# Latent attention in another order: 512 latent columns token tile by token tile, rope keys under the norm, values behind the scores

## The chip, the cores and the metric

The kernel runs on one core of one Trainium2 chip. The metric is the device time of one execution in microseconds (us), lower is better. Three runs of the kernel before took 2278.98, 2285.95 and 2294.7 us, median 2285.95. All work is in fp32: a product with a weight is written as three matmuls on split operands, so that the weights need two passes of other engines before they can be used.

## The reference

Two stacks of transformer layers stand behind each other, over 256 tokens of width 1024. The change touches one mixer alone, the latent attention (MLA) in the third layer of the second stack, between one MLP and the next:

```python
H, dqk = MLA_HEADS, MLA_NOPE + MLA_ROPE            # 8 heads, 128 + 64
c_q, c_kv, k_pe = jnp.split(x @ w_in, [384, 384 + 256], axis=-1)
q = (rms_norm_2(c_q, q_norm_g) @ w_uq).reshape(B, S, H, dqk)
q = jnp.concatenate([q[..., :MLA_NOPE], rope(q[..., MLA_NOPE:], positions)], -1) * (dqk ** -0.5)
kv = (rms_norm_2(c_kv, kv_norm_g) @ w_ukv).reshape(B, S, H, MLA_NOPE + MLA_V)
k_nope, v = kv[..., :MLA_NOPE], kv[..., MLA_NOPE:]
k_pe = rope(k_pe[:, :, None, :], positions)
...
s = jnp.einsum('bqhd,bkhd->bhqk', qi, k)           # causal mask, softmax, then p @ v
return o.reshape(B, S, H * MLA_V) @ w_o            # 1024 x 1024
```

The result is added to ALPHA times the layer's input and goes through a layer norm, whose output the next MLP reads.

## The kernel before

Every engine has its own program, written out by hand; the order in it is the order of execution, and semaphores join the engines. 256 tokens are two token tiles of 128 (`tt`).

**Weights.** Five slots of 128 x 2048 fp32 go round as a ring. SyncE (SP) loads them in one queue, in the order of use, each as soon as PE has released the slot's user five places earlier (`slot_free`). ScalarE (ACT) writes a rounded copy `slot_hi` (L1242), VectorE (DVE) the remainder `slot_lo` (L1612), and only then may PE read it. Both engines do that in line with their other work, at calls of `weights.ahead(u)`: everything up to three slots past `u` is split there, and an engine that comes to it before the load has landed waits, with all that stands behind it.

**Banks.** PE writes into four PSUM banks, also a ring. The order of `bank(...)` calls in `plan()` says which product gets which bank; a bank can be opened only when its user four places earlier has been read out. Sums of down projections go into a separate accumulator `acc`.

**Products.** `product` (L676) is three matmuls: hi x hi, hi x lo, lo x hi. A matmul has 256 or 512 columns. `transposes` and the like (L674) are PE transposes against the identity. PE's `wait` and `in_sbuf` first let the array run empty if a slot is still to be released.

**The latent attention before.** The input projection's 640 latent columns and 64 rope columns come as three slots `mw`: number 2 (192 columns and the rope columns twice), then 0 and 1 (256 columns each). `head` does 2 and 0 token tile by token tile, because the layer norm ahead delivers them so; then PE makes the rope keys feature-major (`mk`), then number 1 (`token_major`). ACT copies all three banks, squares, and DVE scales 384 and 256 columns (L2222 to L2229) in one go. PE transposes five latent tiles (`mc`), DVE multiplies them by the gain into `mcg` (L2236), ACT rounds (L1570), DVE subtracts (L2242): `mcT`. Then four slots `muq` give queries (`mq` 0 to 3 plain, 4 and 5 rope), two slots `mukv` keys and values (`mkv`). DVE turns the rope parts in `exchanged` (L2073 to L2076) straight out of the bank, which holds that bank. Then 8 heads' scores (`ms`), mask and maximum on DVE (L1682 to L1688), exponentials on ACT (L1303), transposes of the probabilities (`mp`), probabilities x values (`my`), division on DVE (L2278), transposes `mt`, and the output projection `mwo` into `acc`. `project` does the first slot over both token tiles and the last three token tile by token tile, so that the next layer norm can start on tile 0; between them stand that norm's transposes (`ln_turned`).

In SP's queue the two tables of the next layer norm (L586) stand between `mw` and `muq`; they wait until the layer norm ahead is over.

## Time and profile before

| what | value |
|---|---|
| runs | 2278.98, 2285.95, 2294.7 us |
| profiled execution | 2281.16 us, of it span 2279.4 us |
| PE busy | 2163.3 us, 95% of the span |
| DVE, ACT, POOL busy | 1394.7, 1095.3, 140.3 us |
| mean granted TensorE clock | 0.984 |
| DMA | 378.10 MB, mean 166 GB/s |

The latent attention lies between about 1554 us and 1694 us of the span. To read it: look at a stretch's granted clock first (1.00 is 2.4 GHz, 0.50 is 1.2 GHz), then at how much of the stretch PE was busy, then at who ended PE's idle time. A share of busy time over the whole span says little here, since all but this stretch runs nearly without gaps.

### The profile page before, as it was taken

What the parts mean: (1) busy time and instruction counts of PE and PEld (TensorE: products, weight loads), DVE (VectorE), ACT (ScalarE), POOL (GpSimd) and SP (SyncE); (2) the same over time, 40 slices, a digit from 0 to 9 for tenths busy, and PEclk for the clock granted to TensorE, in tenths of its full rate; (3) what the DMA queues carried; (4) which work ended last, traced back from release to release, by engine and by line L of the source; (5) the groups of instructions that cost most, each with busy time, mean ns of one, the idle gap of its engine ahead of it and who ended that gap; (6) DMA issues with size and microseconds to landing.
All of it is one profiled execution on the core that took longest, in us unless ns stands there. A gap on an engine that the chain in (4) does not pass through costs nothing.

```text
span 2279.4 us, 33795 instructions
## 1 busy us (share of the span) xinstructions
PE 2163.3 (95%) x14753; PEld 1991.5 (87%) x14759; DVE 1394.7 (61%) x1477; ACT 1095.3 (48%) x1254; POOL 140.3 (6%) x82
## 2 busy tenths in 40 slices
PE   7998999999999999999999889997889999999998
PEld 6988899899889999988998879997679989988997
DVE  5856677675667666555655676555546557465654
ACT  4565555546545543444544654443335434354443
POOL 1000010020001003100000100000000003000000
PEclk9999999999999999999999999998899999999999
DMA  7423555563345555554555545563325565445553
GB/s 234 158 93 130 166 185 194 166 199 93 111 167 174 187 166 194 163 167 160 191 185 185 188 131 185 185 205 114 111 94 184 187 202 184 163 154 178 185 185 130
DMA packets 273292, 378.10 MB, mean 166 GB/s; under 512 B 13957, under 2 KB 236410, under 8 KB 273146
## 3 DMA queue, kind: packets, MB, share of 16 engines
q1 hardware_dynamic: 272236, 374.57, 50.3%
q8 instruction: 117, 1.92, 0.4%
q10 hardware_dynamic: 910, 1.38, 0.2%
q14 instruction: 29, 0.24, 0.0%
HBM read 374.87 MB, written 1.05 MB: 165 GB/s over the span
## 4 chain that ended last, share of the span: by engine, by line
PE 80%; DVE 7%; ACT 4%; DMA 3%; DVEq 2%; issue 1%; PEld 1%; SPq 1%; POOL 0%; ACTq 0%; PEldq 0%; POOLq 0%
PE bank L676 51%; PE acc L676 27%; DVE slot_lo L1612 3%; PE bank L674 2%; DVEq L1607 2%; ACT slot_hi L1242 1%; DMA slot<-in_w_in 1%; PEld bank L676 1%; DMA slot<-in_lru_w_in 1%; ACT arena L1237 1%; SPq L551 0%; DVE arena L2168 0%; DVE split L1645 0%; ACT split L1270 0%; DVE arena L1951 0%
## 5 line engine op out<-in xcount | busy, mean ns | idle before, releaser
L1612 DVE TENSOR_TENSOR slot_lo<-slot,slot_hi 128x2048 fp32r<-128x2048 f32 (+1 forms) x344 | 807.0, 2351 | 436.7 <-ACT slot_hi L1242 435.7
L676 PE MATMUL bank<-split,slot_hi 128*128 128x256 f32 x5496 | 1008.5, 286 | 15.3 <-ACT arena L1237 5.6
L676 PEld LDWEIGHTS bank<-split,slot_hi 128*128 128x128 f32 x5496 | 869.0, 193 | 29.5 <-issue 10.7
L1242 ACT ACTIVATE slot_hi<-slot 128x2048 fp32r<-128x2048 f32 (+1 forms) x344 | 653.0, 1902 | 303.4 <-DMA slot<-in_mlp_w 145.5
L676 PE MATMUL bank<-split,slot_lo 128*128 128x256 f32 x2748 | 781.1, 284 | 0.0
L676 PE MATMUL acc<-slot_hi,split 128*128 128x512 f32 x1904 | 610.4, 393 | 16.7 <-DVE split L2207 8.3
L676 PEld LDWEIGHTS bank<-split,slot_lo 128*128 128x128 f32 x2748 | 530.9, 193 | 0.0
L676 PEld LDWEIGHTS acc<-slot_hi,split 128*128 128x128 f32 x1904 | 359.8, 189 | 95.8 <-issue 8.5
L676 PE MATMUL acc<-slot_lo,split 128*128 128x512 f32 x952 | 373.1, 392 | 0.0
L676 PE MATMUL bank<-slot_hi,split 128*128 128x256 f32 (+1 forms) x1648 | 309.1, 287 | 20.6 <-DVE split L1645 11.7
L1237 ACT ACTIVATE arena<-bank 128x512 f32<-128x512 f32 (+1 forms) x194 | 108.8, 574 | 391.3 <-PE bank L676 359.8
L676 PEld LDWEIGHTS bank<-slot_hi,split 128*128 128x128 f32 x1648 | 262.5, 194 | 25.4 <-DVE split L1645 14.6
L676 PE MATMUL bank<-slot_lo,split 128*128 128x256 f32 (+1 forms) x824 | 236.0, 286 | 0.0
L676 PEld LDWEIGHTS acc<-slot_lo,split 128*128 128x128 f32 x952 | 180.0, 189 | 34.1
L676 PEld LDWEIGHTS bank<-slot_lo,split 128*128 128x128 f32 x824 | 159.9, 194 | 0.8
L676 PE MATMUL bank<-arena 128*128 128x64 f32 (+7 forms) x596 | 112.1, 353 | 18.1 <-ACT arena L1237 8.2
L676 PEld LDWEIGHTS bank<-arena 128*128 128x128 f32 (+2 forms) x596 | 80.3, 202 | 41.9 <-issue 30.6
L2005 DVE TENSOR_TENSOR arena<-arena 128x512 f32<-128x512 f32 x64 | 44.2, 691 | 112.3 <-ACT arena L1237 112.1
L1951 DVE SCALAR_TENSOR_TENSOR arena<-bank,par,arena 128x254 f32<-128x254 f32 (+1 forms) x176 | 76.7, 478 | 52.4 <-ACT arena L1407 49.1
L1407 ACT ACTIVATE arena<-bank,par 128x256 f32<-128x256 f32 x88 | 44.8, 560 | 97.5 <-PE bank L676 92.7
L1703 DVE TENSOR_TENSOR split<-arena,split 128x512 fp32r<-128x512 f32 x86 | 59.0, 686 | 26.7 <-ACT split L1417 20.4
L674 PE MATMUL bank<-con,arena 128*128 128x128 f32 x302 | 46.3, 301 | 21.7 <-DVE arena L1799 8.7
(194 smaller groups left out, 1038.5 us busy)
## 6 DMA issues: line engine op xcount, KB each, us to landing
slot<-in_mlp_w SPq DMA_DIRECT2D x128, 1024.0 KB, 5.4
slot<-in_ret_w_in SPq DMA_DIRECT2D x48, 1024.0 KB, 5.2
slot<-in_w_up SPq DMA_DIRECT2D x44, 1024.0 KB, 5.1
slot<-in_w_in SPq DMA_DIRECT2D x42, 1024.0 KB, 5.3
slot<-in_w_down SPq DMA_DIRECT2D x22, 1024.0 KB, 5.0
slot<-in_ret_w_o SPq DMA_DIRECT2D x16, 1024.0 KB, 5.1
slot<-in_lru_w_in SPq DMA_DIRECT2D x10, 1024.0 KB, 8.1
slot<-in_w_out SPq DMA_DIRECT2D x8, 1024.0 KB, 6.1
```

The lines of the kernel that those rows point to most:

```text
L674: i = nc.tensor.transpose(o, w, ident)
L676: i = nc.tensor.matmul(o, w, m, start=start, stop=stop)
L1237: return A(o, i, func, **kw).then_inc(bank_read[u.r], 1)
L1242: A(whi[u.r][:, 0:u.cols], raw[u.r][:, 0:u.cols], ACT.Copy).then_inc(slot_hi[u.r], 1)
L1407: i = A(cgv[:, 2 * (s % 2) + j, gv, :], bank[u.r][:, j * S:(j + 1) * S], ACT.Identity, scale=par[:, L, PF_CW + 4 * FFT + f:PF_CW + 4 * FFT ...
L1607: dve.drain()
L1612: TTO(wlo[u.r][:, 0:u.cols], raw[u.r][:, 0:u.cols], f32(whi[u.r][:, 0:u.cols]), ALU.subtract)\
L1703: TTO(hid[1][:, r, :, :], hq[:, r, :, :], f32(hid[0][:, r, :, :]), ALU.subtract)\
L1951: i = STT(out=y, in0=bank[u.r][:, j * S:(j + 1) * S - sh], scalar=par[:, L, PF_CW + (2 - sh) * 2 * FFT + f:PF_CW + (2 - sh) * 2 * FFT + f ...
L2005: TTO(h, h, h, ALU.mult).then_inc(V["product_ready"], 1)
```

## The change

It is an order and nothing else is computed:

- `mw` is loaded as two half matrices, rows 0 to 511 and 512 to 1023 of the first 512 columns, and the third slot as before (128 latent columns, rope columns), now last. `wide_head` gives one token tile of 512 columns per bank.
- The norm of the first 384 columns runs as soon as those are there; the third slot's columns, transposes of three latent tiles and the rope keys are computed meanwhile. The last two latent tiles are transposed after the first `muq`. The gain is applied by ACT and DVE directly on the bank; `mcg` is gone.
- The rope parts are copied out by ACT (L1237 before) and turned by DVE in SBUF.
- The keys of both `mukv` slots come first, then all scores, and the values of each half behind them. Half 1's values and transposes stand around half 0's outputs; `mt` 2 and 3 behind the first slot of the output projection.
- ACT copies half of the values. The places of `weights.ahead` in ACT's and DVE's programs move accordingly.

```diff
     rows("ln3", 0)
+    slot("mw", [0, 1])
+    bank("mw", [0])
+    rows("ln3", 1)
+    bank("mw", [1])
     slot("mw", [2], dmas=2)
-    slot("mw", [0])
-    bank("mw", [2, 0])
-    rows("ln3", 1)
+    bank("mw", [2])
+    bank("mc", [0, 1])
     bank("mk", [0])
-    slot("mw", [1])
-    bank("mw", [1])
-    bank("mc", range(3))
-    for f in range(3):
+    for f in range(5):
         his.take("mc", f)
     for i in range(4):
         slot("muq", [i], 3 * 2 * (NOPE + ROPE), dmas=4)
-        bank("mq", [i])
-        if i % 2 == 0:
-            bank("mq", [4 + i // 2])
-    slot("mukv", [0])
-    bank("mkv", [0, 1, 4, 6])
-    slot("mukv", [1])
-    bank("mkv", [2, 3, 5, 7])
-    bank("ms", range(4))
-    bank("ms", range(4, 8))
+        bank("mq", ([0, 4], [1], [2, 5], [3])[i])
+        if i == 0:
+            bank("mc", [2])
+    slot("mukv", range(2))
+    bank("mkv", range(4))
+    bank("ms", range(8))
+    bank("mkv", [4, 6])
     bank("mp", range(4))
     bank("my", range(2))
+    bank("mkv", [5, 7])
     bank("mp", range(4, 8))
+    bank("mt", range(2), True)
     bank("my", range(2, 4))
-    bank("mt", range(4), True)
+    bank("mt", range(2, 4), True)
     slot("mwo", range(4))
     layer_norm(4)
     mlp(2)
...
             u, w = slots["mw", 2], I["mla_w_in_2"][0]
+            for i in range(2):
+                put(slots["mw", i], half(w, 0, i))
             load(u, part(u, 256, 0, w, QR + 128, 192), part(u, 256, 192, w, QR + KVR, ROPE))
-            for c in range(2):
-                put(slots["mw", c], columns(w, c * 256))
...
+            def half_rows(u, o, tt, i, end=None):
+
+                w = [part[u.r][:, :].rearrange("p (k n) -> p k n", n=512) for part in (whi, wlo)]
+                for k in range(4):
+                    product(o[:, :], lambda a: hT[a][:, 4 * i + k, tt * P:(tt + 1) * P], lambda a: w[a][:, k, :],
...
+            def wide_head(name, turned, us, bs):
+
+                for tt in range(TT):
+                    if tt:
+                        turned(1)
+                    o, end = open_bank(bs[tt])
+                    for i, u in enumerate(us):
+                        if tt == 0:
+                            arrived(u)
+                        evacuated(pe, banks[name, (tt, i)])
+                        half_rows(u, o, tt, i, end)
+                        if tt:
+                            freed(u)
...
+            wide_head("ln3", ln_turned(3), [slots["mw", i] for i in range(2)], [banks["mw", tt] for tt in range(TT)])
             u = slots["mw", 2]
-            head("ln3", ln_turned(3), [(slots["mw", c], banks["mw", c]) for c in (2, 0)], held=(u,))
+            arrived(u)
+            o, end = open_bank(banks["mw", 2])
+            for tt in range(TT):
+                token_rows(u, o, tt, end if tt else None)
...
+            wait(V["cn_ready"], 1)
+            latents((0, 1), 0)
+            latents((2,), 1)
             o, end = open_bank(banks["mk", 0])
...
             freed(u)
-            token_major(slots["mw", 1], banks["mw", 1])
-            wait(V["cn_ready"], 1)
-            for i in range(3):
-                transposes(banks["mc", i], mcn, 2 * i, 2 if i < 2 else 1)
             wait(V["mcT_ready"], 3)
...
                 if i % 2 == 0:
-                    turned, turned_end = open_bank(banks["mq", 4 + i // 2])
-                for k in range(3):
-                    product(turned[:, (i % 2) * S:(i % 2 + 1) * S],
-                            lambda a: w[a][:, k, 2 * NOPE:3 * NOPE],
-                            lambda a: mcT[a][:, k, :], k == 0, k == 2, turned_end if (i % 2, k) == (1, 2) else None)
+                    straight()
+                    both = open_bank(banks["mq", 4 + i // 2])
+                    turning(*both)
+                else:
+                    turning(*both)
+                    straight()
                 freed(u)
+                if i == 0:
+                    wait(V["cn_ready"], 2)
+                    latents((3, 4), 2)
+            wait(V["mcT_ready"], 5)
...
-            for g in range(2):
+            def mla_transposes(g):
                 wait(V["mla_probs"], g + 1)
                 for j in range(4):
                     prob_transposes("mp", banks["mp", 4 * g + j], sc2[:, g, j, :])
-                in_sbuf("mp", range(4 * g, 4 * g + 4))
...
+            def mla_weighted(g):
+                opened = [open_bank(banks["my", 2 * g + tt]) for tt in range(TT)]
+                in_sbuf("mkv", [4 + g, 6 + g])
+                for j in range(4):
+                    h = 4 * g + j
+                    in_sbuf("mp", [h])
+                    for tt in range(TT):
+                        o, end = opened[tt]
...
+            def mla_turned(g):
+                in_sbuf("my", [2 * g, 2 * g + 1])
+                for i in (2 * g, 2 * g + 1):
+                    transposes(banks["mt", i], y2, 2 * i)
+
+            def mla_ready(c):
+                if c == 1:
+                    mla_turned(1)
+                in_sbuf("mt", [c])
+
+            wait(V["rot_out"], 10)
+            in_sbuf("mq", range(4))
+            in_sbuf("mkv", range(2))
+            softmax_scores("ms", range(4), mla_pairs)
+            wait(V["rot_out"], 11)
+            in_sbuf("mkv", range(2, 4))
+            softmax_scores("ms", range(4, 8), mla_pairs)
+            mla_values(0)
+            mla_transposes(0)
+            mla_weighted(0)
+            mla_values(1)
+            mla_transposes(1)
+            mla_turned(0)
+            mla_weighted(1)
+            project("mwo", 4, yT2, mla_ready, ln_turned(4))
...
-            weights.ahead(slots["mw", 2])
+            weights.ahead(slots["mw", 0])
+            for tt in range(TT):
+                u = banks["mw", tt]
+                full(act, u)
+                copy(mc[:, tt, 0:512], bank[u.r][:, :], u)
+                evacuated(act, u)
+                last = A(mcsq[:, tt, 0:QR], mc[:, tt, 0:QR], ACT.Square, accum_out=col(C_SSQ + tt))
+            last.then_inc(V["ckv_squared"], 1)
+            act.wait_ge(V["ckv_var"], 1)
+            A(col(C_STD, 2), col(C_VAR, 2), ACT.Sqrt).then_inc(V["ckv_std"], 1)
+            weights.ahead(slots["mw", 1])
+
...
+            latents(range(3))
             u = banks["mw", 2]
             full(act, u)
             copy(mc[:, :, 512:640], bank[u.r][:, :].rearrange("p (t n) -> p t n", t=TT)[:, :, 0:P], u)
-            for c in range(2):
-                weights.ahead(slots["mw", c])
-                copies("mw", c, mc[:, :, c * 256:(c + 1) * 256])
-            for c in range(3):
...
+            u = banks["mk", 0]
+            full(act, u)
+            copy(mkp[:, :], bank[u.r][:, 0:S], u)
+            weights.ahead(slots["mw", 2])
             for i in range(4):
-                weights.ahead(slots["muq", i])
+                if i % 2:
+                    copies("mq", 4 + i // 2, mqr[:, i - 1:i + 1, :])
                 copies("mq", i, mqn[:, 2 * i:2 * i + 2, :])
-            for g in range(2):
-                weights.ahead(slots["mukv", g])
-                for i in (2 * g, 2 * g + 1):
-                    copies("mkv", i, mkn[:, 2 * i:2 * i + 2, :])
-            for g in range(2):
+                if i == 0:
+                    latents((3, 4))
+                if i < 3:
+                    weights.ahead(slots["muq", i])
+            for i in range(4):
...
+            mla_exps(0)
+            weights.ahead(slots["mukv", 0])
+            values_out(0)
+            mla_exps(1)
+            values_out(1)
...
-            for i in range(4):
+            for i in range(2):
                 hi_part("mt", i, yT2)
-            project("mwo", 4)
+            weights.ahead(slots["mukv", 1])
+            weights.ahead(slots["mwo", 0])
+            for i in range(2, 4):
+                hi_part("mt", i, yT2)
+            for c in range(1, 3):
+                weights.ahead(slots["mwo", c])
...
-            def exchanged(u, i, out, n):
-
-                full(dve, u)
-                w = out.shape[-1] * (out.shape[1] if len(out.shape) == 3 else 1)
+            def exchanged(a, i):
+
+                w = a.shape[1] * S
...
-                    TTO(of(mtm[:, 2 * i + 1, :], to), of(bank[u.r], r), table(sin4, r), ALU.mult)
-                TTO(of(mtm[:, 2 * i, :]), of(bank[u.r]), table(cos4), ALU.mult).then_inc(bank_read[u.r], 1)
+                    TTO(of(mtm[:, 2 * i + 1, :], to), a[r, :, :], table(sin4, r), ALU.mult)
+                TTO(of(mtm[:, 2 * i, :]), a, table(cos4), ALU.mult)
                 d()
-                TTO(out if len(out.shape) == 3 else out.rearrange("p (a s) -> p a s", s=S), of(mtm[:, 2 * i, :]),
-                    of(mtm[:, 2 * i + 1, :]), ALU.add).then_inc(V["rot_out"], 1)
+                TTO(a, of(mtm[:, 2 * i, :]), of(mtm[:, 2 * i + 1, :]), ALU.add).then_inc(V["rot_out"], 1)
...
+            normed(0, 0, QR)
+            weights.ahead(slots["mw", 1])
+            latents(range(3))
+            normed(1, QR, KVR)
+            weights.ahead(slots["mw", 2])
+            latents((3, 4))
+            weights.ahead(slots["muq", 0])
+            evacuated(dve, banks["mk", 0])
+            exchanged(mkp.rearrange("p (a s) -> p a s", s=S), 1)
+            weights.ahead(slots["muq", 1])
+            evacuated(dve, banks["mq", 4])
+            exchanged(mqr[:, 0:2, :], 0)
+            weights.ahead(slots["muq", 2])
+            evacuated(dve, banks["mq", 5])
+            exchanged(mqr[:, 2:4, :], 1)
...
+            mla_max(0)
+            weights.ahead(slots["muq", 3])
+            mla_max(1)
+            values_out(0)
+            mla_divisors(0)
...
+            mla_out(0)
+            weights.ahead(slots["mukv", 0])
+            values_out(1)
+            mla_divisors(1)
+            for i in range(2):
                 lo_part("mt", i, yT2)
-            project("mwo", 4)
+            mla_out(1)
+            weights.ahead(slots["mukv", 1])
+            weights.ahead(slots["mwo", 0])
+            for i in range(2, 4):
```

Three places where it moves rows. First **ACT behind the layer norm ahead**: `slot_52` is the first `muq` slot, `arena<-bank` the copies of the `mw` banks. Before:

```order
L1242 ACTIVATE slot_hi<-slot_52 128x1152
L1237 ACTIVATE arena<-bank 128x2x128
L1242 ACTIVATE slot_hi<-slot_53 128x1152
L1237 ACTIVATE arena<-bank 128x2x256
L1242 ACTIVATE slot_hi<-slot_49 128x1152
L1237 ACTIVATE arena<-bank 128x2x256
L1562 ACTIVATE arena,stat<-arena 128x384 x2
L1562 ACTIVATE arena,stat<-arena 128x256 x2
L1565 ACTIVATE stat<-stat 128x4
L1570 ACTIVATE split<-arena 128x512 x2
L1570 ACTIVATE split<-arena 128x256
```

and now:

```order
L1323 ACTIVATE slot_hi<-slot_52 128x1152
L1318 ACTIVATE arena<-bank 128x512
L1638 ACTIVATE arena,stat<-arena 128x384
L1318 ACTIVATE arena<-bank 128x512
L1638 ACTIVATE arena,stat<-arena 128x384
L1641 ACTIVATE stat<-stat 128x2
L1323 ACTIVATE slot_hi<-slot_53 128x1152
L1649 ACTIVATE split<-bank,parg 128x256 x3
L1318 ACTIVATE arena<-bank 128x2x128
L1658 ACTIVATE arena,stat<-arena 128x256 x2
L1661 ACTIVATE stat<-stat 128x2
```

The first split of a `muq` slot still stands ahead of every copy; the squares of the first 384 columns stand behind one `muq` split instead of three.

Second **DVE from the first turned rope queries to the scores** (`slot_51` and `slot_52` in the second piece are the two `mukv` slots; L2185 to L2188 are L2073 to L2076 of before). Before:

```order
L2073 TENSOR_TENSOR arena<-bank,trig 32x512 x4
L2074 TENSOR_TENSOR arena<-bank,trig 128x512
L2076 TENSOR_TENSOR arena<-arena 128x512
L1612 TENSOR_TENSOR slot_lo<-slot_52,slot_hi 128x2048
L1612 TENSOR_TENSOR slot_lo<-slot_53,slot_hi 128x2048
L2073 TENSOR_TENSOR arena<-bank,trig 32x512 x4
L2074 TENSOR_TENSOR arena<-bank,trig 128x512
L2076 TENSOR_TENSOR arena<-arena 128x512
L1612 TENSOR_TENSOR slot_lo<-slot_49,slot_hi 128x2048
L2253 COPY arena<-bank 128x512 x2
L1612 TENSOR_TENSOR slot_lo<-slot_50,slot_hi 128x2048
L2253 COPY arena<-bank 128x512 x2
```

and now:

```order
L1725 TENSOR_TENSOR slot_lo<-slot_51,slot_hi 128x2048
L2185 TENSOR_TENSOR arena<-arena,trig 32x512 x4
L2186 TENSOR_TENSOR arena<-arena,trig 128x512
L2188 TENSOR_TENSOR arena<-arena 128x512
L1725 TENSOR_TENSOR slot_lo<-slot_52,slot_hi 128x2048
L2185 TENSOR_TENSOR arena<-arena,trig 32x512 x4
L2186 TENSOR_TENSOR arena<-arena,trig 128x512
L2188 TENSOR_TENSOR arena<-arena 128x512
L1795 TENSOR_TENSOR arena<-bank,con 128x384 x4
L1797 TENSOR_REDUCE stat<-arena 128x4
L1798 TENSOR_REDUCE stat<-arena 128x4
L1801 TENSOR_SCALAR stat<-stat 128x8
```

The turning reads `arena` instead of a bank, each `mukv` split stands ahead of one turning, and the copies of the values are gone from between the splits and the scores' masks.

Third **ACT from the exponentials to the next layer norm**. Before:

```order
L1303 ACT_TABLE_LOAD
L1303 ACTIVATE arena,stat<-arena,stat 128x128 x4
L1303 ACTIVATE arena,stat<-arena,stat 128x256 x4
L1303 ACTIVATE arena,stat<-arena,stat 128x128 x4
L1303 ACTIVATE arena,stat<-arena,stat 128x256 x4
L1237 ACTIVATE arena<-bank 128x384 x4
L1311 ACTIVATE split<-bank 128x512 x4
L1242 ACTIVATE slot_hi<-slot_51 128x2048
L1242 ACTIVATE slot_hi<-slot_52 128x2048
```

and now:

```order
L1384 ACT_TABLE_LOAD
L1384 ACTIVATE arena,stat<-arena,stat 128x128 x4
L1384 ACTIVATE arena,stat<-arena,stat 128x256 x4
L1323 ACTIVATE slot_hi<-slot_49 128x2048
L1318 ACTIVATE arena<-bank 128x512
L1384 ACTIVATE arena,stat<-arena,stat 128x128 x4
L1384 ACTIVATE arena,stat<-arena,stat 128x256 x4
L1318 ACTIVATE arena<-bank 128x512
L1318 ACTIVATE arena<-bank 128x384 x4
L1392 ACTIVATE split<-bank 128x512 x2
L1323 ACTIVATE slot_hi<-slot_50 128x2048
L1323 ACTIVATE slot_hi<-slot_51 128x2048
```

Weight splits and the values' copies stand between the two halves' exponentials, and two more splits between the first and the last two pieces of the projection's input.

## Rows read from the trace of the kernel before

**Rows 1.** The page: the chain that ended last, shares by engine.

```profile
PE 80%; DVE 7%; ACT 4%; DMA 3%; DVEq 2%; issue 1%; PEld 1%; SPq 1%; POOL 0%; ACTq 0%; PEldq 0%; POOLq 0%
```

**Rows 2.** Windows: each stretch, busy time (and instructions) per engine, granted clock, DMA.

```profile
1567.70:1573.00 5.30, 0.31 (x4) 0.11 (x2) 0.32 (x1) 1.44 (x2) 0.00 (x0) 0.91 0.94 225
1573.00:1578.60 5.60, 5.60 (x26) 5.60 (x27) 2.50 (x3) 1.65 (x2) 0.00 (x0) 0.50 0.00 0
1578.60:1584.40 5.80, 5.80 (x48) 5.63 (x46) 2.47 (x7) 1.17 (x1) 0.00 (x0) 0.98 0.74 196
1589.20:1594.00 4.80, 2.39 (x10) 1.99 (x10) 3.65 (x8) 2.52 (x4) 0.00 (x0) 0.50 0.03 9
1594.00:1599.40 5.40, 5.34 (x25) 5.34 (x26) 1.36 (x2) 1.19 (x3) 0.00 (x0) 0.50 0.00 0
1617.20:1623.10 5.90, 5.90 (x15) 4.74 (x16) 3.98 (x4) 0.69 (x1) 0.00 (x0) 0.50 0.00 0
1629.60:1647.80 18.20, 18.18 (x76) 10.70 (x76) 7.15 (x13) 3.61 (x16) 0.00 (x0) 1.00 0.19 59
1651.40:1657.00 5.60, 5.55 (x26) 5.58 (x27) 0.74 (x2) 1.31 (x6) 0.00 (x0) 0.50 0.00 0
1667.40:1671.30 3.90, 3.90 (x10) 3.08 (x11) 3.38 (x2) 2.28 (x2) 0.00 (x0) 0.56 0.00 0
1671.30:1688.70 17.40, 17.30 (x75) 13.63 (x74) 5.98 (x6) 4.71 (x6) 0.00 (x0) 1.00 0.28 81
```

**Rows 3.** Timeline, PE: start, length, matmuls; in brackets idle before and releaser.

```profile
1572.97 0.80 PE L676 MATMUL bank<-split,slot_hi 128*128 128x256 f32 x2 [4.99 <-ACT arena L1237]
...
1589.20 2.39 PE L674 MATMUL bank<-con,arena 128*128 128x128 f32 x10 [4.76 <-DVE arena L2229]
...
1594.06 0.80 PE L676 MATMUL bank<-split,slot_hi 128*128 128x256 f32 x2 [2.47 <-DVE split L2242]
...
1617.18 0.80 PE L676 MATMUL bank<-slot_hi,split 128*128 128x512 f32 x1 [4.04 <-DVE arena L2074]
...
1629.57 10.79 PE L676 MATMUL bank<-arena 128*128 128x128 f32 x41 [0.98 <-DVE arena L2253]
...
1651.45 5.46 PE L676 MATMUL bank<-arena 128*128 128x128 f32 x24 [3.67 <-DVE arena L2272]
...
1659.46 2.92 PE L676 MATMUL bank<-arena 128*128 128x128 f32 x24 [0.95 <-ACT arena L1237]
...
1663.36 1.83 PE L674 MATMUL bank<-con,xn 128*128 128x128 f32 x15 [0.99 <-DVE xn L2278]
...
1667.40 0.57 PE L676 MATMUL acc<-slot_hi,split 128*128 128x512 f32 x1 [2.10 <-DVE split L1622]
...
1690.01 1.32 PE L674 MATMUL bank<-con,x 128*128 128x128 f32 x8 [1.34 <-DVE x L1991]
```

**Rows 4.** Timeline, SP's queue and ACT, around the first wait.

```profile
1564.69 18.10 SPq L504 DMA_DIRECT2D slot<-in_mla_w_uq  x16
...
1571.48 1.16 ACT L1242 ACTIVATE slot_hi<-slot 128x1152 fp32r<-128x1152 f32 x1 [8.00 <-DMA slot<-in_mla_w_uq]
...
1574.27 0.58 ACT L1237 ACTIVATE arena<-bank 128x512 f32<-128x512 f32 x1
...
1598.80 1.90 ACT L1242 ACTIVATE slot_hi<-slot 128x2048 fp32r<-128x2048 f32 x1
```

**Rows 5.** Timeline, DVE, between 1603 and 1620.

```profile
1603.15 2.79 DVE L2073 TENSOR_TENSOR arena<-bank,trig 32x512 f32<-32x512 f32 x4
1605.96 0.69 DVE L2074 TENSOR_TENSOR arena<-bank,trig 128x512 f32<-128x512 f32 x1
...
1617.83 2.29 DVE L1612 TENSOR_TENSOR slot_lo<-slot,slot_hi 128x2048 fp32r<-128x2048 f32 x1
```

**Rows 6.** Timeline, PE, two other places of the same run.

```profile
1017.27 3.14 PE L674 MATMUL bank<-con,arena 128*128 128x128 f32 x24 [0.26 <-issue]
...
1276.65 0.51 PE L676 MATMUL bank<-split,slot_hi 128*128 128x256 f32 x2 [1.70 <-DVE slot_lo L1612]
```

175 lines of the change are left out of this document (86 added, 89 removed).

## The prediction

> **What bounds the kernel now.** I read the chain that ended last first: PE holds 80% of it [rows 1], so what can be gained is PE's idle time and PE's slow time. Then I went through PE's timeline for idle before a row. The latent attention, 1567.7 to 1694 us, has ten waits of 0.9 us or more in sequence [rows 3]: 4.99, 4.76, 2.47, 4.04, 0.98, 3.67, 0.95, 0.99, 2.10 and 1.34 us. Their sum is **26.3 us**. Third the windows, for the clock: behind each long wait the granted clock stands at 0.50, 1.2 GHz [rows 2]. There 25 matmuls of 256 columns take 5.34 us (0.214 each), at 1.00 48 take 5.80 us (0.121 each); with 512 columns, 75 take 17.3 us at 1.00 (0.23 each), where the stretches at 0.50 hold 15 matmuls, most of them of 512, in 5.90 us. PE was busy 2.39 + 5.34 + 5.90 + 5.55 + 3.90 = 23.1 us in the five slow stretches behind the second and later waits; at full clock the same work takes about 0.54 of that, so they cost 0.46 x 23.1 = **10.6 us**. The slow stretch of 5.60 us behind the first wait costs 2.6 us more. Idle plus slow clock without that last one: **36.9 us** in this stage. It is the stock from which the new order can take; no matmul goes away.
>
> **The parts, one by one.**
>
> *First wait (4.99 us): stays.* The row says ACT's copy ended it, but ACT itself stood 8.00 us for the load of the first `muq` slot [rows 4]. That load begins at 1564.69, behind the two norm tables in SP's queue, which is not changed; nor is the split of `muq` 0 ahead of ACT's first copy. The load keeps four transfers in front of `muq`, the same bytes. What is new: the third slot's product wants the bank of token tile 0, whose copy is 512 columns, 0.58 us, behind the split of 1.16 us that begins at 1571.48. So PE resumes at about 1573.2. It comes to the wait some 0.6 us earlier, since tile 1 of 512 columns is 24 x 0.23 = 5.5 us where 48 x 0.121 = 5.8 us stood, and begins a little earlier. The wait becomes 5.9 us, and the slow stretch behind it stays.
>
> *Waits for the norm (4.76 and 2.47 us) and their slow stretches: go.* Squares start behind the first copy, at about 1573.2; before, they stood behind the last product, which ended at 1589.20 - 4.76 = 1584.4, and PE waited bare for copy, squares and scaling. Now PE has the third slot's 48 matmuls meanwhile (about 8 us, since 27 of them run slow). The rope keys, 24 x 0.121 = 2.9 us, cover the gain and the subtraction of the three query latents. The second norm has the same cover plus the first `muq` slot (27 x 0.121 = 3.3 us).
>
> *Wait for the turning (4.04 us): goes, and another comes.* Five DVE rows of before read the bank [rows 5]; now one ACT copy of 0.58 us frees it. But DVE's queue is long there. The second `mukv` slot's split is behind the turning of the first rope queries: PE is through the rope keys at 1573.2 + 8.3 + 0.8 + 2.9 = 1585.2 and through two `muq` at about 1592.4; ACT copies the bank (0.58) and splits the first `mukv` slot (1.90 [rows 4]), to 1595; DVE ends its part at about 1597.4, then turns for 2.79 + 0.69 + 0.69 = 4.2 us and splits for 2.29 us [rows 5], to 1604.0. PE has done four `muq` (13 us from 1585.2) and the first keys at about 1602. So I put **2.0 us** in. Below: 0, if the first `mukv` load lands early; above: 6.5 us, if turning and split lie bare in front of PE. I take 2.0 because every link of that queue has a row of this length. It leaves the clock at 1.00 in my sum: 1.70 us of idle behind dense work was followed by two matmuls in 0.51 us, full speed [rows 6], while 2.10 us behind thin work [rows 3] was followed by a slow stretch.
>
> *Wait for the values (0.98 us) and for the probabilities (3.67 us, with the slow 5.55 us behind it): go for the most part.* Scores take some 16.6 us for 8 heads (PE was busy 18.18 of 18.2 us in the stretch that also holds 12 transposes, about 1.6 us at the pace of [rows 6]) [rows 2]. Exponentials of heads 0 to 3 are ready before the scores of heads 4 to 7 are done, as before; the mask and maximum of heads 4 to 7 end about 2.7 us after PE's last score, which is what the first half's values (12 x 0.23 = 2.8 us) now cover. Left are short waits for banks: 0.4 us for the first probability copy, 0.3 before the second half's last transposes, 0.5 elsewhere. I write **1.2 us**; below 0, above the 3.7 us of the row that it replaces.
>
> *Waits around the output (0.95, 0.99, 2.10 us, and the slow 3.90 us): go.* The first half's `mt` is transposed before the second half's outputs are computed, so rounding and subtraction have those 2.92 us [rows 3] as cover. `mt` 2 and 3 have the first `mwo` slot, 24 x 0.23 = 5.5 us. The two extra weight splits that DVE does there (2 x 2.29 us) fit into that and the next slot.
>
> *The wait of 1.34 us before the next norm's transposes: halves.* It hangs on a load that needs the first `mwo` slot released, and the distance from there to the end of token tile 0 grows by the 8 transposes only. I keep **0.7 us**.
>
> *PE emptying itself.* The new order has more `wait` and `in_sbuf` calls; eight of them come where a slot is to be released, at some 0.15 us each: **1.2 us**. No row shows one alone; below 0, above 0.98 us each (8 us), the shortest wait but two in [rows 3], most of which was the awaited engine.
>
> *Transposes and the clock.* In this run 24 transposes in a row (3.14 us) and eight more behind two short waits ran at the full rate [rows 6]; the whole stretch had clock 1.00. The Trainium skill, TensorE: Matmul & The Clock Gate, Part 4 (PE-mode transpose), says the opposite: transposes do not count as work for the clock. By that rule the new thin stretch would lower the clock, and the sum would be rival A's; the trace differs from it. I sum by the trace: clock 1.00 in the stretch of 40 transposes between 1626 and 1641 us.
>
> **Sum.** Stock 26.3 + 10.6 = 36.9 us. Left over: 5.9 + 2.0 + 1.2 + 0.7 + 1.2 = 11.0 us. Gain **25.9 us**. Against the profiled execution, 2281.2 us with 2279.4 us of span, that is 2255.3 us. Its time is 4.8 us below the median of the three runs; from the median the same gain gives 2260.1. I forecast **2259 us**, near the latter. Behind the stage PE runs without gaps, so nothing downstream takes the gain back.
>
> **Rivals.**
>
> *A. The clock falls in the thin stretch.* For it: a slow stretch followed 2.10 us of idle behind thin work [rows 2, 3], and the new stretch is thin for 15 us. Against: the 24 transposes and what came after them [rows 6]. It is also what the rule of the Trainium skill named above would give. Price, with all of it from about 1626 to 1641 slow and the first part of the output projection too: 12 us of work there takes 0.85 more of itself, 10 us, plus some 1 us more waiting; gain 15, about **2271 us**.
>
> *B. DVE's and ACT's queues, not PE, set the pace from `muq` to the scores.* For it: DVE has two turnings (8.4 us), the rope keys' turning and four splits in one row, and each split waits for ACT and each of ACT's for a load. Price: the wait before the second keys grows from 2.0 to the bare 6.5 us, the clock falls behind it (2.6 us, as behind the first wait), and the second turning holds up the scores of heads 4 to 7 by nothing, as it has 8 us of cover. Gain 19, about **2267 us**.
>
> *C. The first wait shrinks as well.* A load of two half matrices could leave the transfers ahead of `muq` shorter, and the third slot arrives in time anyway. At most 5 us and the slow clock: gain 31 to 33, **2254 us**. Against: the queue position of the tables.
>
> *D. Slower than before.* One mechanism: the clock, once down at 1573 us, does not come back for most of the stage because the new order never gives PE a long dense run. The stage is 126.3 us long; less 26.3 of idle PE is busy for 100 us, or 87 us at full clock. Each us of it that stays slow costs 0.85. From 31 us of such work on, the gain of 26 us is gone; with 58 us, the kernel is over 1% slower; with 75 us it is 38 us slower, about **2324 us**. Against it: each 0.50 stretch of before returned to 1.00 after 4 to 6 us of busy PE, also behind thin work.
>
> *E. Nothing comes of it*: the idle time moves behind the scores into equal waits. Gain under 10, about **2280 us**. Little speaks for it, since four of the seven long waits lose their cause.
>
> **Numbers.** 1% is 22.9 us, about what a measurement of this kernel can tell from no change. Forecast 0.60, A 0.13, B 0.14, C 0.05, D 0.03, E 0.05. The runs before lie 16 us apart, so a median of three wanders by some 4 us; the forecast's own sum of 26 us lies just 3 us above the bound. Of the forecast's 0.60, 0.43 is faster by over 1%; of B 0.05; of C all; of A 0.02; together 0.55. Slower by over 1%: 0.03, D. The rest, 0.42, is within 1%. The range reaches from C's 2254 us less the wandering, 2246 us, to A's 2271 us plus it, 2275 us; outside lie D, E and the ends of the others, about 0.2.
>
> **What would show it.** Right: PE's wait for ACT's copy behind token tile 1 is still there, 5 to 6 us, with a 0.50 stretch behind it; no wait in front of the first six transposes; one wait of about 2 us on a `mukv` split between the second and third key bank; none over 1 us between the scores and the output projection; clock 1.00 there. The stage ends about 26 us earlier. Wrong: a 0.50 stretch between values and output projection (A); a wait over 4 us on DVE's split (B); no wait behind token tile 1 (C); PE busy for more than 100 us in the stage (D).

## The result: 31 us less, and the profile after

The changed kernel took 2251.41 us (median of four runs, 2250.94 to 2252.48); the kernel before, four runs beside it, 2282.47 us. The ratio is 0.9846, 95% interval 0.9828 to 0.9863: faster by 1.5% (31 to 39 us by the interval, 31.1 us by these two medians). The runs of before lie far apart (2278.98 to 2294.7 us), and the quotient of the two medians, 0.9864, lies just outside the interval. The forecast was 2259 us, the range 2246 to 2275. The profiled execution took 2252.48 us, 28.7 us less than that of before.

To leave out what happens elsewhere in the program, I measure the **stage** from PE's first product behind one layer norm (the row with a wait of about 1 us for DVE's `split`) to the same place behind the next. Before it is 139.72 us (1561.97 to 1701.69), after 108.02 us: 31.7 us less. That is 3 us more than the whole profiled difference, because the stage begins 3.2 us later in the execution after than in the one before. One reason can be seen in work that did not change: behind the 24 transposes of [rows 6] the execution after has a slow stretch, where that of before has none:

```profile
1019.79 3.13 PE L680 MATMUL bank<-con,arena 128*128 128x128 f32 x24 [0.26 <-issue]
...
1024.00:1030.00 6.00, 5.27 (x20) 4.13 (x19) 6.00 (x14) 2.79 (x5) 0.00 (x0) 0.72 0.02 7
```

The profiled execution of before is not a usual one. Of 29 further executions of that kernel, 4 took 2279 to 2283 us at a mean granted clock of 0.983 or 0.984, as the profiled one did (2281.16 us, 0.984), and 25 took 2285 to 2291 us at 0.978 to 0.981. A mean clock that is lower by 0.005 over 2280 us is an estimated 23 us more at 1.2 GHz; at the prediction's 0.46 they cost 10 us, enough for the 8.4 us between the medians of the two groups. So the 31.7 us are measured against one of the shorter executions of before. Against the usual ones the gain is some 35 us.

The whole stage as one window. Columns: length, busy us (and instructions) of PE, weight loads, DVE, ACT, POOL, then granted clock, DMA share, GB/s. Before:

```profile
1561.90:1701.70 139.80, 111.95 (x623) 95.31 (x623) 71.59 (x98) 49.81 (x90) 0.00 (x0) 0.88 0.35 108
```

After:

```profile
1565.10:1673.20 108.10, 98.81 (x599) 83.20 (x599) 68.36 (x93) 52.65 (x98) 0.00 (x0) 0.98 0.45 139
```

PE's idle time fell from 27.85 to 9.29 us, by 18.6 us; its busy time fell by 13.1 us although nearly the same work is done, because the clock rose from 0.88 to 0.98. The timeline of PE after, with every idle stretch of the stage (start, length, matmuls; in brackets the idle time before and who ended it). It answers to [rows 3]:

```profile
1565.14 0.47 PE L682 MATMUL bank<-slot_hi,split 128*128 128x512 f32 x1 [1.07 <-DVE split L1758]
...
1575.65 0.55 PE L682 MATMUL bank<-slot_hi,split 128*128 128x256 f32 x1 [4.82 <-ACT arena L1318]
...
1586.65 0.47 PE L682 MATMUL bank<-split,slot_hi 128*128 128x256 f32 x2 [0.26 <-issue]
...
1590.35 0.63 PE L680 MATMUL bank<-con,arena 128*128 128x128 f32 x4 [0.23 <-issue]
...
1600.94 0.47 PE L682 MATMUL bank<-split,slot_hi 128*128 128x256 f32 x2 [0.26 <-issue]
...
1605.72 0.50 PE L682 MATMUL bank<-split,slot_hi 128*128 128x256 f32 x2 [1.68 <-DVE slot_lo L1725]
...
1628.61 1.50 PE L680 MATMUL bank<-con,arena 128*128 128x128 f32 x12 [0.26 <-issue]
1630.38 2.92 PE L682 MATMUL bank<-arena 128*128 128x128 f32 x24 [0.27 <-DVE arena L2397]
...
1636.32 1.50 PE L680 MATMUL bank<-con,arena 128*128 128x128 f32 x12 [0.26 <-issue]
...
1647.24 1.06 PE L680 MATMUL bank<-con,xn 128*128 128x128 f32 x8 [0.23 <-issue]
...
1673.16 0.39 PE L682 MATMUL bank<-slot_hi,split 128*128 128x256 f32 x1 [0.98 <-DVE split L1758]
```

Where `issue` stands in the brackets, the profile shows nothing that was late; in the program PE lets its array run empty there ahead of a wait. Ten waits of 0.9 us or more, 26.3 us, have become two, 4.82 and 1.68 us, and seven short ones of 1.8 us in all: 8.3 us. (The last row's 0.98 us stands in both kernels.) Windows of after, which answer to [rows 2]:

```profile
1575.60:1579.00 3.40, 3.35 (x18) 3.38 (x19) 2.08 (x6) 2.91 (x7) 0.00 (x0) 0.58 0.80 201
1579.00:1583.50 4.50, 4.50 (x41) 4.50 (x40) 1.17 (x1) 0.16 (x1) 0.00 (x0) 1.00 0.20 46
...
1605.70:1626.00 20.30, 20.28 (x91) 12.95 (x92) 12.58 (x18) 9.69 (x21) 0.00 (x0) 1.00 0.00 1
1626.00:1642.00 16.00, 15.21 (x106) 13.21 (x105) 11.10 (x18) 9.94 (x26) 0.00 (x0) 1.00 0.42 133
```

One stretch at 1.2 GHz is left, behind the first wait. The thin stretch from 1626 us, in which 32 of the 106 instructions are transposes, has clock 1.00; the other 8 of the 40 follow at 1647 us. Behind the two waits that are left stand these rows of SP's queue, ACT and DVE of after, which answer to [rows 4, 5]:

```profile
1566.05 0.43 SPq L592 DMA_DIRECT2D tab<-in_ln_b  x1
1566.53 12.34 SPq L503 DMA_DIRECT2D slot<-in_mla_w_uq  x16
...
1573.86 1.16 ACT L1323 ACTIVATE slot_hi<-slot 128x1152 fp32r<-128x1152 f32 x1 [7.30 <-DMA slot<-in_mla_w_uq]
1574.93 0.58 ACT L1318 ACTIVATE arena<-bank 128x512 f32<-128x512 f32 x1
...
1599.21 2.77 DVE L2185 TENSOR_TENSOR arena<-arena,trig 32x512 f32<-32x512 f32 x4
1602.00 0.69 DVE L2186 TENSOR_TENSOR arena<-arena,trig 128x512 f32<-128x512 f32 x1
1602.77 0.69 DVE L2188 TENSOR_TENSOR arena<-arena 128x512 f32<-128x512 f32 x1
1603.38 2.29 DVE L1725 TENSOR_TENSOR slot_lo<-slot,slot_hi 128x2048 fp32r<-128x2048 f32 x1
```

The first wait: ACT stands 7.30 us for the first `muq` load, splits it, and only then copies the bank that PE wants. The second: DVE turns rope queries out of `arena` for 4.2 us and then splits the second `mukv` slot, until 1605.67, and PE goes on at 1605.72.

### The profile page after: what moved, and what is told of

Read it like the earlier page. It is cut to its first block, busy times and chain, and to the rows that moved or that the text cites. A ratio compares the mean times of both kernels' runs of the same rounds, so it can differ in the third digit from the quotient of the medians.

```text
span 2250.7 us, 33710 instructions
## 1 busy us (share of the span) xinstructions
PE 2151.1 (96%) x14705; PEld 1979.4 (88%) x14711; DVE 1391.1 (62%) x1473; ACT 1097.8 (49%) x1262; POOL 142.2 (6%) x82
## 4 chain that ended last, share of the span: by engine, by line
PE 81%; DVE 7%; ACT 4%; DMA 2%; DVEq 2%; issue 1%; SPq 1%; PEld 0%; POOL 0%; ACTq 0%; PEldq 0%; POOLq 0%
PE bank L682 51%; PE acc L682 28%; DVE slot_lo L1725 3%; PE bank L680 2%; DVEq L1720 2%; ACT slot_hi L1323 1%; DMA slot<-in_w_in 1%; DMA slot<-in_lru_w_in 1%; ACT arena L1318 1%; SPq L557 0%; PEld bank L682 0%; DVE arena L2279 0%; DVE split L1758 0%; ACT split L1351 0%; DVE arena L2064 0%
## 5 line engine op out<-in xcount | busy, mean ns | idle before, releaser
L682 PEld LDWEIGHTS bank<-split,slot_hi 128*128 128x128 f32 x5496 | 865.4, 193 | 23.4 <-issue 10.4
L682 PEld LDWEIGHTS bank<-slot_hi,split 128*128 128x128 f32 x1616 | 257.9, 194 | 27.6 <-DVE split L1758 13.3
```

Source lines behind the costliest of these rows:

```text
L682: i = nc.tensor.matmul(o, w, m, start=start, stop=stop)
```

## The experiments

The theory: the stage has got shorter by waits that found cover, each by one move of the change, and by the slow stretches that they had brought; the first wait is a load behind two tables in SP's queue. The rivals: one move made it all, or the moves' covers are interchangeable (a wait taken back is absorbed elsewhere); the clock follows how thin PE's work is and not its idle time. All kernels but one start from the changed one. Kernels that were run together share their runs of the kernel before, whose medians were 2289.51, 2288.81 and 2287.57 us. The stage's length is the finer measure, since it leaves the other 2140 us out; the medians of three sets of runs of the changed kernel differ by 3 us.

**base, base2: the changed kernel again.**

> The changed kernel again, unchanged, as the ruler of this set. Its stage (from the first matmul behind the layer norm ahead to the same place behind the next layer norm) was 108.0 us in the first profile, 139.7 before. Theory (each wait of before lost its cause, and the slow clock went with the waits): 107 to 110 us again, ratio to before 0.983 to 0.987. Rival (part of the gain is chance, since the profiled execution of before had more slow stretches outside the stage too): stage over 112 us or ratio above 0.99.

> The changed kernel a third time, unchanged, for the comparison with the combined version on the same chip. Stage 108 to 109 us, depending on whether the 0.50 stretch behind the first wait lasts 3.4 or 6.8 us.

Measured: 2252.98 us, ratio 0.9849 (0.9828 to 0.9870), stage 109.02 us; and 2254.5 us, ratio 0.9859 (0.9838 to 0.9880), stage 109.41 us. Both have the same waits as after (4.71 and 4.79, 1.68 and 1.68), but a longer slow stretch behind the first. A window of base there:

```profile
1572.10:1578.60 6.50, 6.50 (x35) 6.50 (x36) 3.19 (x6) 2.85 (x7) 0.00 (x0) 0.60 0.60 143
```

So the same kernel, with nearly the same idle time, has about 3 us or 5 to 6 us at the low clock, and its stage is 108.0 or 109.0 to 109.4 us. Differences are taken against 109.0 where the long stretch is there (e1, e2, e3, e5), and against 108.0 otherwise.

**e1: the values back in front of the scores.**

```diff
-    bank("mkv", range(4))
+    bank("mkv", [0, 1, 4, 6, 2, 3, 5, 7])
     bank("ms", range(8))
-    bank("mkv", [4, 6])
     bank("mp", range(4))
     bank("my", range(2))
-    bank("mkv", [5, 7])
...
-            mla_values(0)
             mla_transposes(0)
             mla_weighted(0)
-            mla_values(1)
             mla_transposes(1)
```

The copies of the values move with them, into ACT's program behind the keys' copies and into DVE's around the second turning.

> Undoes one part: the values of each half are computed right behind the keys of that half, ahead of all scores, as before. Theory: PE's wait of 1.68 us on the second key/value slot's split goes (values cover it), and between the scores and the first weighted product a wait of 2.0 to 2.5 us on DVE comes back (before: 3.67, for all four copies; now only the first copy is needed), perhaps with a 0.50 stretch behind it worth 2.5 us. Stage 108.4 to 111.3 us. Rival (the place of the values does not matter, DVE's mask and maximum of the second half are in time anyway): no wait over 1 us there, stage 106 to 107 us. Rival (the values' place carries most of the gain): stage above 115 us.

Measured: 2257.42 us, ratio 0.9868 (0.9844 to 0.9892), stage 110.84 us, +1.8. The wait on `mukv` is gone, since 12 matmuls of 512 columns now stand in front of it. In its place, the timeline of PE of e1:

```profile
1630.31 1.53 PE L678 MATMUL bank<-con,arena 128*128 128x128 f32 x12
1634.42 4.54 PE L680 MATMUL bank<-arena 128*128 128x128 f32 x24 [2.59 <-DVE arena L2410]
```

PE waits 2.59 us for the probabilities, and the 24 matmuls behind it take 4.54 us, where they take 2.92 us after. So the changed order saves 2.6 us of wait and 1.6 us of slow clock here, and pays 1.7 us of wait on the split and some more short emptyings of PE (0.3 us) for it. The same cover serves one place or the other, and the sum is a small gain.

**e2: one norm wait again (squares and gain behind the third slot, rope keys ahead).**

```diff
-    bank("mc", [0, 1])
     bank("mk", [0])
+    bank("mc", [0, 1])
...
-            wait(V["cn_ready"], 1)
-            latents((0, 1), 0)
-            latents((2,), 1)
             o, end = open_bank(banks["mk", 0])
...
             freed(u)
+            wait(V["cn_ready"], 1)
+            latents((0, 1), 0)
+            latents((2,), 1)
             wait(V["mcT_ready"], 3)
```

On ACT the third slot's copy now stands ahead of the squares.

> Undoes one part: ACT squares the first 384 columns only behind the copy of the third slot's product, and PE makes the rope keys ahead of its wait for the norm, as before. Theory: PE waits bare for squares and scaling (1.5 to 2.5 us) and again for gain and subtraction (2.4 us), stage plus 4 to 5 us, and plus 2 to 3 us more if a 0.50 stretch follows: 112 to 116 us. Rival (the later parts have slack that absorbs it, as DVE's queue ends the wait on the key/value split at the same time): the wait of 1.68 us shrinks by the same amount and the stage stays at 108 to 110 us.

Measured: 2259.94 us, ratio 0.9875 (0.9853 to 0.9897), stage 113.05 us, +4.0. The timeline of PE of e2:

```profile
1589.32 0.87 PE L680 MATMUL bank<-con,arena 128*128 128x128 f32 x6 [0.28 <-DVE arena L2339]
...
1592.44 0.51 PE L682 MATMUL bank<-split,slot_hi 128*128 128x256 f32 x2 [2.24 <-DVE split L2347]
```

The wait for rounding and subtraction came back at 2.24 us, near the 2.47 us of [rows 3], and 1.2 us behind it, at about 1593.6 us, the clock fell and stayed low to 1597 (0.65 over 1594.6 to 1598.0). The wait for the norm itself, 4.76 us before, came back at just 0.28 us: the rope keys alone cover it, although the squares start later. That half of my expectation for this kernel was too large.

**e3: the last 16 transposes together, behind all outputs.**

```diff
             mla_transposes(1)
-            mla_turned(0)
             mla_weighted(1)
-            project("mwo", 4, yT2, mla_ready, ln_turned(4))
+            in_sbuf("my")
+            for i in range(4):
+                transposes(banks["mt", i], y2, 2 * i)
+            in_sbuf("mt")
+            project("mwo", 4, yT2, lambda c: None, ln_turned(4))
```

On ACT and DVE the weight splits of this place move behind all four pieces.

> Undoes one part: all 16 output transposes behind the second half's weighted products, with the output projection waiting for all four, as before. Theory: waits of 0.9 to 1.1 us (division) and about 2.1 us (rounding and subtraction) come back, with a 0.50 stretch worth 2 us behind them: stage plus 3 to 5 us, 111 to 113 us. Rival (the clock stays at 1.00 since the stretch ahead is denser than it was): plus 3 us, no 0.50 stretch. Rival (the two weight splits moved behind hold up the next layer norm instead): a wait over 1.5 us before that norm's transposes, stage above 114 us.

Measured: 2257.47 us, ratio 0.9866 (0.9845 to 0.9887), stage 112.96 us, +3.9. The timeline of PE of e3:

```profile
1636.36 2.92 PE L681 MATMUL bank<-arena 128*128 128x128 f32 x24
1640.26 1.94 PE L679 MATMUL bank<-con,xn 128*128 128x128 f32 x16 [0.98 <-DVE xn L2371]
1644.29 0.47 PE L681 MATMUL acc<-slot_hi,split 128*128 128x512 f32 x1 [2.10 <-DVE split L1726]
```

Two waits of before, 0.99 and 2.10 us, are back, at 0.98 and 2.10. But the clock stays at full rate behind the 2.10 us: 24 matmuls of 512 columns follow in 5.70 us at 1.00. In before the same wait stood behind three others close together and was followed by a slow stretch [rows 2]. Idle time makes 3.2 us of the 3.9; for the other 0.8 us, more busy time at full clock, I have no cause.

**e4: the two norm tables behind the `muq` loads in SP's queue.**

```diff
-            layer_norm(4)
             for i in range(4):
                 u, w = slots["muq", i], I["mla_w_uq_2"][0]
...
+            layer_norm(4)
             for g in range(2):
                 put(slots["mukv", g]
```

> Changes what the change left alone: in SP's queue the two tables of the next layer norm stand behind the four query slots instead of ahead of them. Theory (the first wait, 4.7 to 4.9 us, hangs on the first query slot's load, which stands behind the tables, and these wait for the layer norm ahead to end): the load starts about 1550 instead of 1566 us, the wait goes to under 1 us, and the 0.50 stretch behind it too (1.9 to 2.6 us): stage 101 to 103 us instead of 108 to 109. Rival (the load itself is late for its size, or its slots are released late): wait of 3 us or more remains, stage above 106 us. Rival (the wait is ACT's own, copy behind a late weight split of the third slot): wait about 2 us, stage 105 us.

Measured: 2248.0 us, ratio 0.9820 (0.9805 to 0.9835), stage 101.79 us, 7.2 us less than base. The first wait and its slow stretch are gone. SP's queue in e4:

```profile
1553.33 20.64 SPq L503 DMA_DIRECT2D slot<-in_mla_w_uq  x16
1574.01 0.48 SPq L592 DMA_DIRECT2D tab<-in_ln_g  x1
```

The loads begin 12 us ahead of the first product of the stage, instead of 1.4 us behind it. Two transfers of tables that only the norm at the stage's end reads had held them up, since the layer norm ahead still read the tables' buffer (after, SP's queue stood 13.2 us for DVE there). This shows the cause of the first wait, which the prediction had named.

**e5: the rope queries turned straight out of the bank, as before.**

```diff
-                    TTO(of(mtm[:, 2 * i + 1, :], to), a[r, :, :], table(sin4, r), ALU.mult)
-                TTO(of(mtm[:, 2 * i, :]), a, table(cos4), ALU.mult)
+                    TTO(of(mtm[:, 2 * i + 1, :], to), src[r, :, :], table(sin4, r), ALU.mult)
+                last = TTO(of(mtm[:, 2 * i, :]), src, table(cos4), ALU.mult)
+                if u is not None:
+                    last.then_inc(bank_read[u.r], 1)
```

`src` is the bank; ACT's copy of `mq` 4 and 5 falls away.

> Undoes one part: the rope queries are turned by DVE straight out of their bank, without ACT's copy; DVE's order stays. Theory (the copy by ACT is what frees the bank in time): PE waits about 4 to 5 us for the bank of the second rope queries, until DVE has turned the first ones; the wait of 1.68 us on the key/value split behind it goes, and a 0.50 stretch worth 2 us may follow: stage plus 2.5 to 6 us, 111 to 115 us. Rival (DVE's place in the queue, not the bank, was the cause of the 4.04 us of before): PE's waits stay as they are, stage 108 to 109 us.

Measured: 2262.98 us, ratio 0.9886 (0.9871 to 0.9901), stage 115.59 us, +6.6: the dearest of the four moves, and above what I expected. PE and DVE of e5:

```profile
1606.58 0.80 PE L682 MATMUL bank<-split,slot_hi 128*128 128x256 f32 x2 [6.41 <-DVE arena L2185]
```

```profile
1598.14 1.71 DVE L2184 TENSOR_TENSOR arena<-arena,trig 32x256 f32<-32x256 f32 x4
...
1600.71 2.29 DVE L1723 TENSOR_TENSOR slot_lo<-slot,slot_hi 128x2048 fp32r<-128x2048 f32 x1
1603.03 2.79 DVE L2184 TENSOR_TENSOR arena<-bank,trig 32x512 f32<-32x512 f32 x4
1605.83 0.69 DVE L2185 TENSOR_TENSOR arena<-bank,trig 128x512 f32<-128x512 f32 x1
```

A bank that DVE hands over is free only when DVE's queue has come to it: the rope keys' turning and a weight split stand ahead, and PE's product was done over 10 us earlier. In the changed kernel ACT's copy frees the same bank at 1593.4 us, 1.4 us after the product's end:

```profile
1592.80 0.59 ACT L1318 ACTIVATE arena<-bank 128x512 f32<-128x512 f32 x1
```

The 6.41 us are not the 4.04 us of [rows 3] come back. That wait hung on the second turning. The first one cost PE 0.44 us, PE's and DVE's timeline of before:

```profile
1606.79 0.48 PE L676 MATMUL bank<-split,slot_hi 128*128 128x256 f32 x2 [0.44 <-DVE arena L2074]
...
1616.43 0.69 DVE L2074 TENSOR_TENSOR arena<-bank,trig 128x512 f32<-128x512 f32 x1
```

By `plan()`, what stands between two uses of this bank is now a latent's transposes and two products, where it was three products. Without ACT's copy PE comes there 6.4 us before DVE has read the bank, and the second turning then ends no wait. What took the 4.04 us away by itself was not tested. The 6.41 us also hide the wait on `mukv`, which has gone, and bring their own slow stretch.

**e6: DVE splits the second `mukv` slot ahead of the first turning.**

```diff
+            weights.ahead(slots["muq", 2])
             evacuated(dve, banks["mq", 4])
             exchanged(mqr[:, 0:2, :], 0)
-            weights.ahead(slots["muq", 2])
```

> One step of DVE's order: the second key/value slot's split ahead of the turning of the first rope queries. Theory: PE's wait of 1.68 us goes, the scores start with no new wait (the first turning ends about 1 us before they need it): stage minus 1.4 to 1.7 us, 106.3 to 107.4 us. Rival (the turning then ends late and the wait moves to the scores): a wait of 1 us or more ahead of the scores, stage unchanged.

Measured: 2254.36 us, ratio 0.9852 (0.9835 to 0.9868), stage 106.03 us with the short slow stretch, 2.0 less than after (0.2 of it from a shorter first wait, 4.60 us). The 1.68 us wait is gone and nothing has taken its place. The timeline of DVE of e6: both splits (4.49 us) stand ahead of the turning.

```profile
1596.01 0.43 DVE L2188 TENSOR_TENSOR arena<-arena 128x256 f32<-128x256 f32 x1
1596.35 4.49 DVE L1725 TENSOR_TENSOR slot_lo<-slot,slot_hi 128x2048 fp32r<-128x2048 f32 x2
```

The runs' median can't tell 2 us; the trace can.

**e7: PE kept busy in the first wait by 20 matmuls of zeros.**

```diff
             u = slots["mw", 2]
+            for i in range(20):
+                mm(acc[:, 1, 512:D], zeros[:, 0:P], zeros[:, :], True, True)
             arrived(u)
```

> Measures the price of the slow clock by itself: 20 matmuls of zeros (bf16, 512 columns, 4.6 us at full clock) into the idle accumulator fill PE's first wait; they compute nothing that is used. Theory (the 0.50 stretch behind the wait follows from the idle array and costs what its matmuls take longer): no 0.50 stretch there, stage minus 1.5 to 2.5 us, 106 to 107.5 us. Rival (matmuls of zeros do not hold the clock): the stretch of 3.4 or 6.8 us stays, stage 108 to 109 us. Rival (the filler overruns the wait): stage longer than 109 us.

Measured: 2254.76 us, ratio 0.9846 (0.9829 to 0.9864), stage 107.67 us. The timeline of PE of e7:

```profile
1566.11 4.49 PE L682 MATMUL acc<-zeros 128*128 128x512 bf16 x20
1571.93 0.36 PE L682 MATMUL bank<-slot_hi,split 128*128 128x256 f32 x1 [1.33 <-ACT arena L1320]
```

There is no slow stretch: the first matmul takes 0.36 us where it takes 0.55 after. From the end of the wait to the next emptying of PE it is 9.77 us, against 11.00 in after, 12.08 in base and 12.40 in base2. So the slow clock behind this wait costs 1.2 to 2.6 us, and it is the idle time that brings it: nine profiles with 4.60 to 4.91 us of idle there have the slow stretch, and this one, with 1.33, has none. PE's whole wait is 1.1 us longer than in base (4.49 and 1.33 against 4.71 us), because the load landed later in this execution, where ACT stood 8.17 us for it; the stage is therefore 1.3 us shorter than base's and not 2.3, just outside the 106 to 107.5 us that I expected.

**e8: e4 and e6 together.** The two edits above.

> The changed kernel with both improvements: the norm tables behind the query slots in SP's queue, and the second key/value split ahead of the first turning. Theory (the two waits are independent): 101.8 - 2.0 = 99.8 us, 99.5 to 100.5 us, some 8 to 9 us or 0.35 to 0.40% below the changed kernel. Rival (with the first wait gone the rest of the stage starts earlier and DVE or a load becomes late at another place): a wait of 1 us or more somewhere new, stage 101 to 103 us.

Measured: 2243.6 us, ratio 0.9811 (0.9791 to 0.9831), 10.9 us less than base2 beside it; stage 99.82 us. This is the fastest version. Its stage as a window:

```profile
1563.40:1663.30 99.90, 97.10 (x599) 81.99 (x599) 68.19 (x93) 52.67 (x98) 0.00 (x0) 1.00 0.43 139
```

2.8 us of idle are left. The edits add up: base2's 109.4 less 7.2 and 2.0 us is 100.2.

**e9: the edit of e4 on the kernel before.**

> The kernel before with one step only: the norm tables behind the query slots in SP's queue. Theory (the first wait of 4.99 us and its 0.50 stretch, 2.6 us, hang on that place in the queue whatever order the rest has): stage 132 to 133.5 us instead of 139.7, ratio to before about 0.997. Rival (in the old order ACT's copy stands behind further splits and the wait stays): wait over 3 us, stage above 137 us.

Measured: 2282.49 us (ten runs), ratio 0.9982 (0.9970 to 0.9994), stage 137.09 us instead of 139.72. I had expected some 7 us. The wait of 4.99 us did go, with its slow stretch, and PE's waits in the stage are 7.4 us less in sum. But ACT then stood 6.96 us for the next `muq` slot with the squares queued behind it, so that the norm's waits, 4.76 and 2.47 us, stayed as they were; and in this execution the clock took much of the gain back. The timeline and windows of e9 over the scores:

```profile
1622.56 28.15 PE L676 MATMUL bank<-arena 128*128 128x128 f32 x64 [0.98 <-DVE arena L2253]
```

```profile
1615.00:1624.50 9.50, 8.52 (x49) 6.77 (x47) 4.44 (x5) 2.48 (x3) 0.00 (x0) 1.00 0.42 152
1624.50:1659.00 34.50, 32.11 (x84) 19.38 (x84) 11.18 (x20) 7.22 (x32) 0.00 (x0) 0.51 0.06 19
...
1629.60:1647.80 18.20, 18.20 (x40) 9.67 (x40) 4.77 (x8) 3.61 (x16) 0.00 (x0) 0.50 0.00 0
```

In before, the same 64 instructions of scores took:

```profile
1629.57 16.75 PE L676 MATMUL bank<-arena 128*128 128x128 f32 x64 [0.98 <-DVE arena L2253]
```

PE was busy without a gap in both, yet e9 has 0.50 and 40 instructions in a window that holds 76 in before [rows 2]. The clock had come back to 1.00 behind the long waits, at about 1615 us. It fell 2 us into the scores, behind the same 0.98 us of idle as in before, and stayed low for 34 us, 26 of them scores without a gap. The scores alone cost 11.4 us more. Over the whole stage PE's busy time is 5.2 us longer than before (117.15 against 111.95), since other slow stretches are gone, and its idle time 7.9 us less: the net of 2.7 us. What decides that the clock falls here and not there is open.

This comparison sets a profile with a mean clock of 0.979 against one with 0.984. The runs allow a fairer one: e9's ten have 0.978 to 0.981 and a median of 2282.49 us; the 12 of before beside them with the same clock have 2288.2, 5.7 us more, which is close to what I had expected. So it may be that usual executions of before have this slow stretch too. No profile of one was taken.

**e10: e1, e2, e3 and e5 together, on the changed kernel.**

> Undoes four parts at once: values ahead of the scores, norm behind the third slot's copy with the rope keys ahead of PE's wait, output transposes in one go, rope queries turned out of the bank. Kept: 512 latent columns per token tile, the gain applied on the bank, two norms, keys of both slots in a row, the places of most splits. Singly they cost 1.8, 4.0, 3.9 and 6.6 us against a stage of 109.0. Theory (the waits add, since PE is the chain between them): 109.0 + 16.3 = 125.3, 123 to 128 us; the remaining 12 to 16 us to the 139.7 of before belong to what is kept. Rival (undone together they bring each other out, as longer idle brings more slow clock): 133 us or more. Rival (they share waits): under 120 us.

Measured: 2271.22 us, ratio 0.9932 (0.9909 to 0.9954), stage 127.00 us. Alone they cost 1.8, 4.0, 3.9 and 6.6 us, 16.4 in sum before rounding; together 19.0 us, taken against 108.0, since e10 has the short slow stretch at the start. Its long waits, PE's timeline:

```profile
1589.14 0.80 PE L679 MATMUL bank<-split,slot_hi 128*128 128x256 f32 x2 [2.24 <-DVE split L2345]
...
1606.64 0.80 PE L679 MATMUL bank<-split,slot_hi 128*128 128x256 f32 x2 [6.41 <-DVE arena L2183]
...
1646.87 3.52 PE L679 MATMUL bank<-arena 128*128 128x128 f32 x15 [2.59 <-DVE arena L2403]
1656.78 1.39 PE L677 MATMUL bank<-con,xn 128*128 128x128 f32 x11 [1.14 <-DVE xn L2387]
1660.82 0.47 PE L679 MATMUL acc<-slot_hi,split 128*128 128x512 f32 x1 [2.10 <-DVE split L1731]
```

The same waits as alone, to the hundredth in most rows: the waits that the four reversals bring stand in series on PE and do not absorb each other. The 2.6 us beyond the sum have two parts. PE's idle time grows by 12.5 us, against 10.7 in the sum of the four: e1 and e5 each removed the 1.68 us wait on `mukv`, and together they can remove it only once. Its busy time grows by 6.5 us against 5.7, which is the clock: over the 10.4 us behind the 6.41 us wait it is 0.71 in e10 and 0.79 in e5. The rival by which one move made it all is refuted, and covers are interchangeable only for that one wait. The other 12.7 us up to before's 139.7 belong to what all these kernels keep: 512 columns per token tile with two norms instead of one, the gain on the bank, the keys in one row, and the places of the weight splits. These I did not take apart.

## Why the prediction was right, point by point

By its terms, against the stage of the two profiles. The waits are 26.3 - 8.3 = 18.0 us less, where I had 26.3 - 11.0 = 15.3. The slow stretches behind the later waits, 10.6 us, are gone as I had it. The one behind the first wait costs 1.2 us (e7) instead of 2.6: 1.4 us, where I had 0. The stage has 24 matmuls fewer (24 of 512 columns for 48 of 256), worth 0.3 us by [rows 2]'s paces, which I had used only inside the first wait. That makes 30.3 of the 31.7 us. Of the rest, 0.5 us are short waits of before that I had not counted (0.44 us at 1606.79 the longest). PE's busy time bears the clock's part out as a whole: 10.6 + 1.4 + 0.3 = 12.3 us against 13.1 measured.

- *First wait stays*: right; e4 shows its cause. 4.82 us instead of 5.9: SP's queue came to the load 1.4 us behind the stage's start (before: 2.7), so ACT's split began 8.7 us behind it (before: 9.5), and PE came to the wait 0.3 us later than I had it. The slow stretch behind it is right in kind and varies in size.
- *Norm waits go*: right, both 0. e2 shows that the cover for the second of them, 2.24 us and its slow stretch, is what counts; for the first the rope keys alone would have done. The slow stretches behind them are gone too: the clock is 1.00 from 1579 us on.
- *A wait of 2.0 us on the second `mukv` split*: right in place, releaser and size (1.68), e6 shows its cause. The clock stays up behind it, in all seven profiles that have this wait, but my ground for that was weak: the row of [rows 6] with 1.70 us of idle stands in all 14 profiles, and in four of them (idle 1.78 to 2.12 us) the clock falls behind it. It was the term with the longest chain of links, and each had a row.
- *The turning*: the 4.04 us are gone, as I had it, but I had the reason only in part. e5 shows that ACT's copy is worth 6.6 us in the new order, for a wait on the other rope bank, that of the first turning.
- *Values behind the scores*: bank waits 0.27 us instead of 1.2. The mis-sizing: I took short waits as likely where cover (2.8 us) and need (2.7 us) were nearly equal, and the cover was enough. e1 shows the move's worth.
- *Output waits go*: right, all 0; e3 gives back 3.9 us.
- *The next norm's wait halves*: mis-sized, it is 0 instead of 0.7.
- *PE emptying itself*: six emptyings at 0.23 to 0.26 us, 1.5 us, where I put eight at 0.15, 1.2 us. I wrote that no row shows one alone; the first row of [rows 6] does, with 0.26 us.
- *Transposes and the clock*: the clock was 1.00 in the thin stretch, as I had it, and here luck had a part. My ground was what followed the 24 transposes of [rows 6]. That place stands unchanged in all 14 profiles, with two waits of 0.73 to 0.74 us behind the transposes, and in six of them, after included, the clock falls behind it.
- *2259 us against 2251.4*: in the stage the gain is 5.8 us above my 25.9. The leftover was 11.0 us where 8.3 stand, the first slow stretch and the matmuls saved 1.7 us more, 0.5 us are the uncounted short waits, and 0.9 us stay open. The mis-sized terms lie nearly all on one side, since I had put each unseen cost above zero. The rest is the start: most executions of before are some 8 us longer than the profiled one, at a lower mean clock, so that a gain read from its stage is too small.

**Rival A**, the clock falls in the thin stretch: refuted by the 1.00 in the window from 1626 us, in after and in every experiment that keeps the order (nine profiles). The Trainium skill's rule in TensorE: Matmul & The Clock Gate, Part 4 (PE-mode transpose), by which transposes do not count as work, is not borne out by this stretch; but 74 other instructions stand among its 32 transposes, so it is no test of transposes alone. Nor is the length of the idle time alone a rule: the clock fell behind 2.59 us in e1 and 2.24 us in e2 and stayed behind 1.68 us in after and 2.10 us in e3, but it fell behind the same 2.10 us in before, behind 0.98 us in e9, and behind the transposes of [rows 6] in six profiles of 14. **Rival B**: the wait on DVE's split was 1.68 us and not 6.5. **Rival C**: not by the change, but its time, 2254 us, is nearer than mine, and e4 shows that the first wait can be had, by moving one line. **Rival D**: refuted for the changed kernel; e9 shows that its mechanism exists, on the old order. **Rival E**: refuted by the timeline of after, which has no wait over 0.27 us between the scores and the next norm.

## What to carry to other kernels

When PE holds 80% of the chain, list its idle stretches in a stage and what the engine that ends each has in its queue, and price a new order by what cover each wait gets; waits in series on one engine add up (16.4 us one by one, 19.0 us together), but look for a wait that two changes both remove. Hand a bank back by the engine that is free, not by the one that needs the data (6.6 us for one extra copy of 0.59 us), and put early weight splits ahead of work whose reader comes later. In a queue with one order, look at what a waiting transfer holds up behind it: moving two small tables gave 7.2 us here. And before a stage of one profile is used as the size of a loss, see whether that execution's time and clock are usual for the kernel: here they were not.

## What the runs showed of the hardware

- The clock's fall behind a given wait differs from execution to execution: about 3 us or 5 to 6 us at 1.2 GHz behind 4.7 to 4.8 us of idle, for the same program (1.2 to 2.6 us of time).
- It also falls or not at one and the same place: behind 24 transposes and two waits of 0.73 to 0.74 us in six of 14 profiles, behind one wait for a split in four of 14 (it fell at 1.78, 2.02, 2.03 and 2.12 us and stayed at 1.81 us and at 1.46 to 1.73 us).
- It can fall within dense work, 2 us behind 0.98 us of idle, and stay low over it: 34 us in e9, with 28.15 us for scores that take 16.75 us at full clock, where all other slow stretches of the stage were over within some 10 us.
- Twenty matmuls of zeros in bf16 kept the clock up through a 5.8 us wait, of which 1.33 us stayed idle (e7).
- Thirty-two transposes among 106 instructions in 16 us left it at 1.00 (after); that stretch has 1.00 in nine profiles.
- A wait on PE that empties the array first costs 0.23 to 0.26 us in most rows even where nothing is late (0.47 us at one place of e1 and e10).
